# One core, two transformer blocks in float32: expert gate/up products from split operands, a shorter ring for the down weights, and an earlier copy in the attention loop

## The reference, cut to what matters

```
for e in range(N_EXPERTS):                                   # 32
    a = jax.nn.silu(h @ w_gate_e[e]) * (h @ w_up_e[e])       # 1024 -> 256, twice
    y = y + gates[:, e:e + 1] * (a @ w_down_e[e])            # 256 -> 1024
return y
```

```
s = jnp.where(valid, jnp.einsum('...', q, k) * HD ** -0.5, NEG)
pr = jax.nn.softmax(s, axis=-1)
o = jnp.einsum('...', pr, v)
```

## Time and profile before

| what | us |
| --- | --- |
| median of 3 runs (lowest, highest) | 2382.17 (2379.54, 2385.83) |
| the profiled execution | 2389.93 |
| its span, first to last instruction | 2388.2 |
| PE busy | 2117.3 (89% of the span) |
| DVE busy | 962.7 (40%) |
| ACT busy | 595.8 (25%) |
| the 16 DMA engines, mean rate | 113 GB/s |
| expert loop, first to last product of gate and up | 500.0 to 832.5 |
| mean clock of PE, as a share of full speed | 0.930 |

### The profile page before, as it was taken

One profiled execution on the slowest core, in us unless ns is written; L12 is line 12 of the kernel. 1 busy time (PEld: TensorE's weight loads), 2 busy tenths in 40 slices (PEclk: granted clock), 3 DMA queues, 4 the chain that ended last, 5 costly groups with the idle time before them and its releaser, 6 DMA issues. The chain is left out here.

```text
span 2388.2 us, 24926 instructions
## 1 busy us (share of the span) xinstructions
PE 2117.3 (89%) x8645; PEld 1435.0 (60%) x8645; DVE 962.7 (40%) x1735; ACT 595.8 (25%) x1122; POOL 112.9 (5%) x175
## 2 busy tenths in 40 slices
PE   3986788379999959889999999998989999999995
PEld 1542544344444435677478887885567657888784
DVE  1554952221111156772523222334866242222335
ACT  1121321011111112244223332221244222333221
POOL 2000000201011010000100000001000000000001
PEclk7996999589999978988999999999899899999998
DMA  8307012258877561001103334224000211333320
GB/s 271 118 0 277 7 54 89 90 209 313 322 303 304 217 237 42 1 19 71 62 18 89 104 88 140 80 89 145 1 1 19 97 53 36 105 88 112 109 97 35
DMA packets 154638, 269.43 MB, mean 113 GB/s; under 512 B 12225, under 2 KB 109681, under 8 KB 141361
## 3 DMA queue, kind: packets, MB, share of 16 engines
q1 hardware_dynamic: 147696, 258.46, 30.8%
q0 software_dynamic: 6848, 9.77, 1.4%
HBM read 257.64 MB, written 23.14 MB: 118 GB/s over the span
## 5 line engine op out<-in xcount | busy, mean ns | idle before, releaser
L231 PE MATMUL bank<-ht_hi,gate_up_hi 128*128 128x512 f32 x704 | 274.1, 389 | 2.9 <-ACT arena L1218 2.9
L232 PE MATMUL bank<-ht_lo,gate_up_hi 128*128 128x512 f32 x704 | 273.9, 389 | 0.0
L233 PE MATMUL bank<-ht_hi,gate_up_lo 128*128 128x512 f32 x704 | 273.9, 389 | 0.0
L1985 PE MATMUL bank<-arena 128*128 128x512 f32 x512 | 226.9, 596 | 3.7 <-DVE arena L1527 3.7
L2045 PE MATMUL bank<-arena 128*128 128x512 f32 (+3 forms) x640 | 199.1, 473 | 8.1 <-ACT arena L1111 7.4
L2045 PEld LDWEIGHTS bank<-arena 128*128 128x128 f32 x640 | 118.6, 203 | 85.6 <-issue 74.7
L1985 PEld LDWEIGHTS bank<-arena 128*128 128x128 f32 x512 | 95.6, 192 | 112.2 <-issue 108.2
L231 PEld LDWEIGHTS bank<-ht_hi,gate_up_hi 128*128 128x128 f32 x704 | 132.2, 188 | 31.2 <-issue 3.8
L233 PEld LDWEIGHTS bank<-ht_hi,gate_up_lo 128*128 128x128 f32 x704 | 132.2, 188 | 27.6
L232 PEld LDWEIGHTS bank<-ht_lo,gate_up_hi 128*128 128x128 f32 x704 | 132.2, 188 | 27.1
L231 PE MATMUL bank<-down_hi,product_hi 128*128 128x512 f32 x352 | 138.2, 392 | 3.5 <-DVE arena L1732 3.5
(11 more groups left out here) (319 smaller groups left out, 3088.4 us busy)
## 6 DMA issues: line engine op xcount, KB each, us to landing
gate_up_whole<-w_gu SPq DMA_DIRECT2D x88, 512.0 KB, 5.0
arena<-w_gate_e SPq DMA_DIRECT2D x32, 1024.0 KB, 4.9
arena<-w_up_e SPq DMA_DIRECT2D x32, 1024.0 KB, 7.6
arena<-w_down_e SPq DMA_DIRECT2D x32, 1024.0 KB, 9.7
arena<-w_ada SPq DMA_DIRECT2D x12, 2048.0 KB, 12.2
down_whole<-w_down SPq DMA_DIRECT2D x44, 512.0 KB, 3.5
arena<-w_in SPq DMA_DIRECT2D x4, 2048.0 KB, 14.8
arena<-w_o SPq DMA_DIRECT2D x2, 4096.0 KB, 14.1
```

The source lines that it names most:

```text
L231: pe.matmul(ps, xh, wh, start=start, stop=False)
L232: pe.matmul(ps, xh, wl, start=False, stop=False)
L233: return pe.matmul(ps, xl, wh, start=False, stop=stop)
L1985: ins = pe.matmul(bank[s % 2][:], XW[s % 2][:, c], ring[s][:, :, c], start=c == 0, stop=c == C8 - 1)
```

## The change

Four things change.

1. The expert's gate and up weights are split as in the feed-forward part, in two halves of four chunks. ACT rounds a half to `ring_hi` (two buffers in all), DVE writes the rest over the weights' own slot (`ring_lo`), and PE makes 24 products where 8 float32 matmuls were. The window is split as well, by two DVE instructions.
2. The loads are taken apart. Gate and up keep a ring of four, refilled when PE has finished the gate/up product of the old expert (`m_half`); the down weights get a ring of two.
3. Expert 0 is split before the sorted rows are transposed; the rest is split two experts ahead, from inside `step`.
4. In the attention, ACT makes `take_pt(n - 3)` ahead of the exponentials of unit n, not behind.

```
-SLOT = C8 * 2 * FE + 2 * D
+GU, DN = C8 * 2 * FE, 2 * D
...
-        ring = [at(base + n * SLOT, 2, C8, FE) for n in range(4)]
-        ring_d = [at(base + n * SLOT + C8 * 2 * FE, 2, D) for n in range(4)]
-        stage = [at(base + 3 * SLOT, T, D), H]
-        Yin = at(base + 4 * SLOT, T, 2, D)
-        off = base + 4 * SLOT
+        ring = [part(f"expert_gate_up{n}", base + n * GU, 2, C8, FE, dt=F32) for n in range(4)]
+        ring_lo = [part(f"expert_gate_up_lo{n}", base + n * GU, 2, C8, FE) for n in range(4)]
+        ring_d = [at(base + 4 * GU + n * DN, 2, D) for n in range(2)]
+        ring_hi = [part(f"expert_gate_up_hi{n}", base + 4 * GU + 2 * DN + n * (GU // 2), 2, C8 // 2, FE) for n in range(2)]
+        stage = [at(base + 3 * GU, T, D), H]
+        off = base + 5 * GU + 2 * DN
+        Yin = at(off, T, 2, D)
...
+        XW_hi = [part(f"window_hi{n}", H0 + T * D + 2 * n * C8 * P, C8, P) for n in range(2)]
+        XW_lo = [part(f"window_lo{n}", H0 + T * D + (2 * n + 1) * C8 * P, C8, P) for n in range(2)]
+        AT = gate_a[:, 0:4 * P].rearrange("p (s c m) -> p s c m", s=2, c=2)
...
-            def load_expert(n, s):
+            def load_gate_up(n, s):
                 for k, w in enumerate(("w_gate_e", "w_up_e")):
-                    sp.dma_start(ring[s][:, k], i[w][0][bass.ds(n, 1)].rearrange("a (p c) n -> (a p) c n", c=C8)).then_inc(s_w[s], 16)
-                sp.dma_start(ring_d[s], i["w_down_e"][0][bass.ds(n, 1)].rearrange("a (p c) n -> (a p) c n", c=2)).then_inc(s_w[s], 16)
+                    sp.dma_start(ring[s][:, k], i[w][0][bass.ds(n, 1)].rearrange("a (p c) n -> (a p) c n", c=C8)).then_inc(s_gu[s], 16)
+
+            def load_down(n, s):
+                sp.dma_start(ring_d[s], i["w_down_e"][0][bass.ds(n, 1)].rearrange("a (p c) n -> (a p) c n", c=2)).then_inc(s_dn[s], 16)
 
             u1.read(sp, ("oT", 0))
-            load_expert(2, 2)
+            load_gate_up(2, 2)
+            load_down(0, 0)
+            load_down(1, 1)
             u1.read(sp, ("mix", T - 1, 1))
-            load_expert(0, 0)
-            load_expert(1, 1)
+            load_gate_up(0, 0)
+            load_gate_up(1, 1)
...
+            load_gate_up(3, 3)
+
+            def refill(n, e, d, s):
+                sp.wait_ge(m_half, 2 * (n - 4) + 2 + 2 * M_CREDIT)
+                load_gate_up(e, s)
+                sp.wait_ge(m_y, n - 4 + 1 + M_CREDIT)
+                load_down(d, s % 2)
+
             with sp.Fori(1, NE // 4) as it:
                 for s in range(4):
-                    sp.wait_ge(m_y, it * 4 + s - 4 + 1 + M_CREDIT)
-                    load_expert(it * 4 + s, s)
...
+            def gate_up_high(n, it, s, half):
+                act.wait_ge(s_gu[s], 32 * (it + 1))
+                act.wait_ge(m_half, 2 * (n - 1) + half + 1 + 2 * M_CREDIT)
+                act.copy(ring_hi[half], ring[s][:, :, 4 * half:4 * half + 4]).then_inc(m_whi, 1)
+
+            act.sem_inc(m_silu, M_CREDIT)
+            act.sem_inc(m_atc, M_CREDIT)
+            act.sem_inc(m_yb, M_CREDIT)
+            act.sem_inc(m_whi, 2 * M_CREDIT)
+            for half in range(2):
+                gate_up_high(0, 0, 0, half)
...
+            gate_up_high(1, 0, 1, 0)
             silu(0, 0)
+            gate_up_high(1, 0, 1, 1)
             copy_at(0, 0)
+
+            def step(n, g, s, ahead):
+                g2, s2 = (g, s + 2) if s < 2 else (g + 1, s - 2)
+                if ahead:
+                    gate_up_high(n + 2, g2, s2, 0)
+                silu(n + 1, (s + 1) % 4)
+                if ahead:
+                    gate_up_high(n + 2, g2, s2, 1)
+                copy_y(n, g, s)
+                copy_at(n + 1, (s + 1) % 4)
+
             with act.Fori(0, last) as g:
                 for s in range(4):
-                    silu(g * 4 + s + 1, (s + 1) % 4)
-                    copy_y(g * 4 + s, g, s)
-                    copy_at(g * 4 + s + 1, (s + 1) % 4)
+                    step(g * 4 + s, g, s, True)
...
+                    if n >= 3:
+                        take_pt(n - 3)
                     y_neg.wait(act, l, n + 1)
                     if n >= 4:
                         u2.evacuated(act, ("pT",) + UNITS[n - 4], l)
@@ -1183,8 +1223,6 @@
                                            scale=HD ** -0.5, accum_out=ls2[:, kk, t, h:h + 1]), ("s", kind, t, h))
                     if n < T - 2:
                         take_in(n + 2, 4)
-                    if n >= 3:
-                        take_pt(n - 3)
                     if n in TURN_AT:
                         key = TURNED[TURN_AT[n]]
...
+            def gate_up_low(n, s, half):
+                dve.wait_ge(m_whi, 2 * n + half + 1 + 2 * M_CREDIT)
+                c4 = slice(4 * half, 4 * half + 4)
+                dve.tensor_tensor(ring_lo[s][:, :, c4], ring[s][:, :, c4], ring_hi[half].bitcast(F32), ALU.subtract).then_inc(m_wlo, 1)
+
+            dve.sem_inc(m_wlo, 2 * M_CREDIT)
+            for half in range(2):
+                gate_up_low(0, 0, half)
...
             def window(e, s):
 
                 w0 = dve.value_load(win[0:1, bass.ds(e, 1)], min_val=0, max_val=2 * S)
-                dve.tensor_copy(XW[s % 2], XsT[:, :, bass.ds(w0, P)]).then_inc(m_xw, 1)
+                dve.tensor_copy(XW_hi[s % 2], XsT[:, :, bass.ds(w0, P)]).then_inc(m_xh, 1)
+                dve.wait_ge(m_xh, e + 1 + M_CREDIT)
+                dve.tensor_tensor(XW_lo[s % 2], XsT[:, :, bass.ds(w0, P)], XW_hi[s % 2].bitcast(F32), ALU.subtract).then_inc(m_xw, 1)
 
             def product(n, s):
                 dve.wait_ge(m_silu, n + 1 + M_CREDIT)
                 dve.wait_ge(m_at, n - 2 + 1 + M_CREDIT)
                 dve.tensor_tensor(A[:, s % 2], SG[:, s % 2], bank[s % 2][:, FE:], ALU.mult).then_inc(m_a, 1)
-                window(n + 2, s)
...
+            gate_up_low(1, 1, 0)
             product(0, 0)
+            gate_up_low(1, 1, 1)
+            window(2, 0)
+
+            def step(n, g, s, ahead):
+                if ahead:
+                    gate_up_low(n + 2, (s + 2) % 4, 0)
+                product(n + 1, (s + 1) % 4)
+                if ahead:
+                    gate_up_low(n + 2, (s + 2) % 4, 1)
+                window(n + 3, s + 1)
+                copy_ya(n, g, s)
+
             with dve.Fori(0, last) as g:
                 for s in range(4):
-                    product(g * 4 + s + 1, (s + 1) % 4)
-                    copy_ya(g * 4 + s, g, s)
+                    step(g * 4 + s, g, s, True)
...
             def gate_up(n, it, s):
                 pe.wait_ge(m_xw, n + 1 + M_CREDIT)
-                pe.wait_ge(s_w[s], 48 * (it + 1))
                 pe.wait_ge(m_a, n - 2 + 1 + M_CREDIT)
-                for c in range(C8):
-                    ins = pe.matmul(bank[s % 2][:], XW[s % 2][:, c], ring[s][:, :, c], start=c == 0, stop=c == C8 - 1)
-                ins.then_inc(m_gu, 1)
+                for half in range(2):
+                    pe.wait_ge(m_wlo, 2 * n + half + 1 + 2 * M_CREDIT)
+                    for c in range(4 * half, 4 * half + 4):
+                        ins = split_product(pe, bank[s % 2][:], (XW_hi[s % 2][:, c], XW_lo[s % 2][:, c]),
+                                            (ring_hi[half][:, :, c % 4], ring_lo[s][:, :, c]), c == 0, c == C8 - 1)
+                    ins.then_inc(m_half, 1)
...
-            def down(n, s):
+            def down(n, it, s):
                 pe.wait_ge(m_atc, n + 1 + M_CREDIT)
+                pe.wait_ge(s_dn[s % 2], 16 * (2 * it + s // 2 + 1) + D_CREDIT)
                 pe.wait_ge(m_ya, n - 2 + 1 + M_CREDIT)
                 pe.wait_ge(m_yb, n - 2 + 1 + M_CREDIT)
                 for half in range(2):
                     for c in range(2):
-                        ins = pe.matmul(bank[4 + 2 * (s % 2) + half][:], AT[:, s % 2, c], ring_d[s][:, c, 512 * half:512 * half + 512],
+                        ins = pe.matmul(bank[4 + 2 * (s % 2) + half][:], AT[:, s % 2, c], ring_d[s % 2][:, c, 512 * half:512 * half + 512],
```

More of the change, by code:

```diff
@@ L451, in build @@
         idx_now = route(4, dt=I32)
+        SG = route(2, FE)
+        A = route(2, FE)
         offB = base
@@ L617, in build @@
         s_pad = sem("xs_pad")
-        s_w = [sem(f"expert_weights{n}") for n in range(4)]
-        m_xw = sem("window_copied")
-        m_gu = sem("gate_up_done")
+        s_gu = [sem(f"expert_gate_up_loaded{n}") for n in range(4)]
+        s_dn = [sem(f"expert_down_loaded{n}") for n in range(2)]
+        m_xh = sem("window_high")
+        m_xw = sem("window_split")
+        m_whi = sem("expert_high_parts")
+        m_wlo = sem("expert_low_parts")
+        m_half = sem("gate_up_halves_done")
         m_silu = sem("silu_done")
@@ L1956, in _ @@
                 u1.full(ins, ("logit", t))
+            pe.sem_inc(m_half, 2 * M_CREDIT)
+            pe.sem_inc(m_at, M_CREDIT)
+            pe.sem_inc(m_y, M_CREDIT)
+            for x in s_dn:
+                pe.sem_inc(x, D_CREDIT)
             pe.wait_ge(s_masks, 1)
@@ L2019, in _ @@
```

(4 more changed lines are left out.)

37 lines of the change are left out of this document (15 added, 22 removed).

## The result

Four runs of the changed kernel took 2310.42 to 2314.97 us, median **2311.51 us**; before on the same chip 2382.14 us (2379.54 to 2385.83, four runs). The ratio is **0.9705, 95% interval 0.9688 to 0.9722**: 70.6 us less, where 55.5 were forecast.

A forecast was written before the change was run, and what follows sets the result against it. PE was taken to bound the expert loop, with DMA close behind. 43.5 us from 30 experts plus 12 from the attention copy made 55.5 off 2389.9: 2334.4, or 2327 us as median; range 2313 to 2350.

The forecast's parts named there:

- The gate/up product: Expert loop: 24 split products at 0.226 us take 5.42 us instead of 6.87; an expert takes 9.08 us, 1.45 less.
- DVE and ACT fit: Expert loop: ACT's work of about 5.6 us and DVE's of 8.4 to 9.0 stay hidden within 9.08 us.
- DVE does bind: Rival, expert loop: DVE becomes the bound, up to 9.8 us an expert and 2348 us in all; chance 0.22.
- Loads and the ring of two: Expert loop: loads need 8.3 us an expert, hidden; down weights have 14.7 us to land. Slower by the ring: chance 0.04.
- The start: Experts 0 and 1: window 1.2 us later, up to 2.4 us of idle PE; the shorter products' gain is lost.
- The copy ahead of the exponentials: Attention loops: moving ACT's copy removes PE's waits before the values, 12 us won; rival of no gain, chance 0.12.
- The upper bound is the whole 19.8: Attention loops: the copy's move can win at most PE's 19.8 us of waits before the values, in both layers.
- the prediction's signs: Changed profile: among others, an expert each 9.1 us, DVE at 0.85 to 0.95, no wait of the values for the copy.
- the low end of the range: Whole kernel: 2313 us, if all 19.8 us of attention waits go and PE's clock gives some 5 us.
- some 5 us: Attention loops: gain from PE keeping its clock where it fell to 0.83, counted only for the range's 2313 us end.
- Where PE was full nothing is won: Attention loops: the copy's move gains nothing in stretches where PE was already full.

The follow-up runs named there:

- the late order with fillers: Changed kernel with the copy put back behind the exponentials, plus unread PE matmuls in units 0-37 and 48-63 of each attention layer: 2335.25 us, ratio 0.9803.

## Why the prediction was wrong in its size, and right in its steps but one

**The gate/up product: right.** 9.13 us for an expert where 9.08 was worked out; the spacing of 0.226 us held for two runs of 256 columns. The stage gave 41.5 us of 43.5.

**DVE and ACT fit: right.** DVE's work is 7.60 us (7.62 with the friendly durations of the earlier trace rows), the cast costs what the copy did, the load of the position nothing. That is below the 8.4 to 9.0 that I took, and DVE is busy for 0.79 of the loop where I had 0.85 to 0.95. With 2.29 us more DVE does bind.

**Loads and the ring of two: right.** PE never waits for them in the loop; they would bind at 8.55 us (8.3 worked out from 380 GB/s, which had the stores in it).

**The start: nearly right.** The window was ready 1.2 us later, at 501.22 for 499.98. PE's wait in expert 1's chain was 1.90 us (up to 2.4 forecast; it stood ahead of the transposes, for DVE's product), and the first down product came at 517.42 for 517.11: about even, as said.

**The copy ahead of the exponentials: this step failed.** The prediction had: "The upper bound is the whole 19.8. I take 60%, 12 us". Measured were 34.5 us in the profiles (33.8 with this edit alone, 29.5 by its medians): above the bound and more than twice the term by each of these counts. The mechanism was right, the bound was none. Nor did the wait of the values for the copy go, as the prediction's signs had it: 3.8 of 10.1 us stay in the first loop. And the low end of the range was set 1 us below its own terms: 43.5 + 19.8 + 5 off 2389.9 gives 2314, not 2313. Three reasons for the size:

1. *A wait can cost clock as well.* 12.9 us, by the late order with fillers (128.8) against the late order without (136.0, 134.6). The prediction named "some 5 us" of it, and only for the low end of the range. The earlier trace rows had the evidence: the stretch from 1070 to 1080, which I read as "PE is full", has a clock of 0.83. PE is full in the same place of the second layer too, but there at 1.00, and units 32 to 39 take 17.4 us for 18.9. The same transposes in the first layer and the second:
```profile
1070.99 1.48 PE L2117 MATMUL bank<-arena 128*128 128x128 f32 x6
...
1820.59 0.83 PE L2117 MATMUL bank<-arena 128*128 128x128 f32 x6
```
2. *PE's idle rows show less than its waiting.* The waits of its weight loads in the loops of before, first layer and second:
```profile
PEld bank L2128 <- ACT arena L1173: 14.2, 21, 2.0
...
PEld bank L2128 <- ACT arena L1173: 14.1, 23, 2.0
```
28.3 us for the same wait that PE's own rows put at 19.8. A short matmul's record reaches into the pause behind it: in the pair above, the load waits 0.72 us where the matmul shows 0.53.
3. *One stretch stood for all.* I took the slack from 1050 to 1060, which lies in units 24 to 31, where DVE leaves little. There my 60% was rather high: 1.3 us won of 2.8 us waited. But in units 48 to 63 DVE is busy for less than half the time, and the round of the ring above shrinks by the whole wait of 0.53, from 2.31 to 1.77. Units 32 to 63 and what follows gave about three quarters of the order's 10.8 us. "Where PE was full nothing is won" holds for units 40 to 47 alone, full at a clock of 1.00: 18.0 before, 18.3 after.

What stays open: the order's own 21.6 us are more than what left the weight loads' rows, 28.3 - 12.0 = 16.3. The fillers, at 0.5 us a loop, don't explain the other 5 us; where they sat is not shown.

The bound should have been taken from the ring's round in each kind of unit, with and without the exponentials in it, and every stretch with a clock below one counted as time that the edit may give back.

## What to carry to other kernels

Read the granted clock beside the busy share: a window in which PE is full at 0.83 does less than a full one, and a wait removed ahead of it can give back more than its own length. Where engines wait for each other in turn, price an edit by the round of the ring in every phase of the loop, not by the sum of one engine's idle time in one phase. What an in-order engine can do without waiting belongs ahead of what waits.

## What the runs showed of the hardware

**GpSimd's copy beside DVE's subtraction.** A copy of one column of indices took 0.2 us before and 1.75 after, in the groups of before and after:
```profile
L922 POOL COPY arena<-arena 128x1 int32 x32 | 6.3, 195 | 4.4 <-issue 4.3
```
```profile
L943 POOL COPY arena<-arena 128x1 int32 x32 | 56.1, 1753 | 1.0 <-issue 0.9
```
The timeline after has one at 572.07 for 1.94 us; it ends at 574.01, and DVE's subtraction at 571.66 ends at 573.95. The next, at 581.19, ends at 583.13, the subtraction beside it at 583.09. The copy lasts until the subtraction is over. The Trainium skill (SBUF — State Buffer, section Who interferes with whom) has the rule: a DVE instruction with two inputs in SBUF contends with a GpSimd instruction that reads SBUF. The trace agrees. No wait of PE, DVE or ACT in the expert loop names POOL, so it cost nothing here.

**A stretch at half clock outlasts the wait ahead of it.** Behind the 1.82 us wait at 1015.70 the records stay long until about 1025.3; behind the 4.96 us wait ahead of the changed kernel's experts the first twelve products start 0.43 us apart. The same wait of 1.82 us in the second layer brought no such stretch.
